# An mLSTM block's per-head weight subtraction: from VectorE to GpSimd

## The reference, cut to what matters

```
qk = silu(depthwise_conv5(concat[mq, mk]))          # q and k of a head
s  = (q @ k.T) * exp(decay matrix)                  # over chunks, two directions
h  = (s @ v) / max(|den|, exp(-m))                  # forward + backward
y  = rmsnorm(h) * g_mlstm * sigmoid(mo)             # mo = tokens @ w_in[:, o-columns]
```

## Time and profile before

| | us |
|---|---|
| median of 3 runs | 3441.33 |
| lowest, highest | 3435.79, 3441.35 |
| the profiled execution's own time | 3441.02 |
| its span, first to last instruction | 3439.2 |
| PE busy | 3324.5 (97%) |
| DVE busy | 2028.6 |
| ACT busy | 1232.1 |
| POOL busy | 357.2 |

### The profile page before, as it was taken

One profiled execution on the slowest core, in us unless ns is written; L12 is line 12 of the kernel. 1 busy time (PEld: TensorE's weight loads), 2 busy tenths in 40 slices (PEclk: granted clock), 3 DMA queues, 4 the chain that ended last, 5 costly groups with the idle time before them and its releaser, 6 DMA issues.

```text
span 3439.2 us, 42627 instructions
## 1 busy us (share of the span) xinstructions
PE 3324.5 (97%) x16432; PEld 2639.3 (77%) x16432; DVE 2028.6 (59%) x2501; ACT 1232.1 (36%) x1530; POOL 357.2 (10%) x334
## 2 busy tenths in 40 slices
PE   8999999999999998999998999999999999999999
PEld 4777768888887776688885587788887477878887
DVE  4676777555566576565567556465557566364443
ACT  3245443221224445432234433342224333343222
POOL 0000101110011001111112100011112011001000
PEclk9999999999999999999999999999999999999999
DMA  6331123323321222054442122244443132232223
GB/s 276 118 103 59 53 69 123 110 100 131 110 98 66 82 85 72 29 188 169 166 149 80 47 74 83 98 145 174 166 166 115 37 99 68 90 106 89 95 97 110
DMA packets 61017, 369.39 MB, mean 107 GB/s; under 512 B 9224, under 2 KB 9864, under 8 KB 19792
## 3 DMA queue, kind: packets, MB, share of 16 engines
q1 hardware_dynamic: 44544, 274.13, 23.0%
q10 hardware_dynamic: 16336, 93.39, 7.5%
HBM read 354.27 MB, written 2.33 MB: 104 GB/s over the span
## 4 chain that ended last, share of the span: by engine, by line
PE 80%; DVE 12%; ACT 5%; issue 3%; DMA 1%; POOL 0%; ACTq 0%; DVEq 0%; SPq 0%; POOLq 0%
PE pair L691 49%; PE pair L1163 8%; PE pair L842 6%; PE pair L729 2%; PE pair L759 2%; PE pair L1231 2%; PE pair L997 2%; DVE w_lo L2240 1%; PE pair L703 1%; ACT w_hi L1524 1%; PE pair L783 1%; PE pair L1059 1%; DVE mxg L2834 1%; PE pair L1362 1%; PE pair L1215 1%
## 5 line engine op out<-in xcount | busy, mean ns | idle before, releaser
L2240 DVE TENSOR_TENSOR w_lo<-raw,w_hi 128x2048 fp32r<-128x2048 f32 x221 | 506.9, 2294 | 285.2 <-ACT w_hi L1524 279.9
L1524 ACT ACTIVATE w_hi<-raw 128x2048 fp32r<-128x2048 f32 x221 | 421.7, 1908 | 622.6 <-PE pair L691 527.9
L691 PE MATMUL pair<-h_hi,w_hi 128*128 128x512 f32 (+2 forms) x1856 | 595.7, 363 | 5.7 <-DVEq L2222 2.7
L691 PE MATMUL pair<-h_lo,w_hi 128*128 128x512 f32 (+2 forms) x1856 | 594.5, 362 | 0.0
L691 PE MATMUL pair<-h_hi,w_lo 128*128 128x512 f32 (+2 forms) x1856 | 594.2, 362 | 0.0
L691 PE MATMUL pair<-u_hi,w_hi 128*128 128x512 f32 x1116 | 374.1, 371 | 19.1 <-DVE x L2281 10.1
L691 PE MATMUL pair<-u_lo,w_hi 128*128 128x512 f32 x1116 | 372.0, 369 | 0.0
L691 PE MATMUL pair<-u_hi,w_lo 128*128 128x512 f32 x1116 | 371.6, 368 | 0.0
L691 PEld LDWEIGHTS pair<-h_hi,w_hi 128*128 128x128 f32 (+2 forms) x1856 | 309.5, 183 | 67.5 <-issue 7.3
L2503 DVE TENSOR_TENSOR u_lo<-arena,u_hi 128x512 fp32r<-128x512 f32 (+1 forms) x128 | 97.1, 759 | 447.7 <-POOL arena L3047 447.4
L691 PEld LDWEIGHTS pair<-h_hi,w_lo 128*128 128x128 f32 (+2 forms) x1856 | 309.5, 183 | 61.3
(11 more groups left out here) (371 smaller groups left out, 4834.5 us busy)
## 6 DMA issues: line engine op xcount, KB each, us to landing
raw<-in_wt_dram SPq DMA_DIRECT2D x222, 1024.0 KB, 4.8
arena<-in_modw_dram ACTq DMA_DIRECT2D x72, 1024.0 KB, 4.9
arena<-in_modw_dram SPq DMA_DIRECT2D x12, 1024.0 KB, 9.6
raw<-in_modw_dram SPq DMA_DIRECT2D x12, 1024.0 KB, 4.8
arena<-arena SPq DMA_DIRECT2D x136, 64.0 KB, 2.0
arena<-negm_rows_dram ACTq DMA_DIRECT2D x16, 384.0 KB, 4.0
x<-in_xt_dram SPq DMA_DIRECT2D x1, 3072.0 KB, 18.6
arena<-in_fconst_dram ACTq DMA_DIRECT2D x2, 1414.0 KB, 6.4
```

Of the source, the lines that this page charges most:

```text
L691: mm = pe.matmul(pp[p][0:m, lo:hi], a[0:rows, k * width + c0:k * width + c0 + m], b[0:rows, k, lo:hi], start=(k == 0 and i == 0), stop=(k ...
L1524: act.activation(w_hi[slot][:], raw[slot][:], ACT.Copy).then_inc(w_hi_done, 1)
L2240: dve.tensor_tensor(w_lo[slot][:], raw[slot][:], w_hi[slot][:].bitcast(F32), ALU.subtract)\
```

## The change

In each head, the subtraction for the gate tile is done by POOL. DVE skips it (it only counts it, so that its later waits have the right values) and, before the `split()` inside the score loop, waits until that of the gate tile is complete. POOL does it first in each head, before its waits for the spread rows and for k. The tile indices are 6, 8, 10 and 12 in layer 0 and 56, 58, 60 and 62 in layer 1. POOL waits for the high part of this tile and for the low parts of all tiles before.

```diff
+            def split_elsewhere():
+
+                t.tile += 1
+                t.next("split")
+                t.next(w_hi_done)
+
...
                     convolve(h, 0)
-                    split()
+                    split_elsewhere()
                     if h:
...
                         if j == (2 if h < MH - 1 else 1):
+
+                            dve.wait_ge(w_lo_done, t.now(w_hi_done, 2))
                             split()
...
+            def split(i):
+
+                pool.wait_ge(w_hi_done, i + 1)
+
+                pool.wait_ge(w_lo_done, i + 2)
+                pool.tensor_tensor(w_lo[i % 2][:], raw[i % 2][:], w_hi[i % 2][:].bitcast(F32), ALU.subtract)\
+                    .then_inc(w_lo_done, 1)
+
             def mlstm(n):
...
                 for h in range(MH):
+                    split(6 + 2 * h if ctx_q else 56 + 2 * h)
 
                     pool.wait_ge(negm_in, t.next(negm_in, 32))
```

## The result

| | median us | lowest, highest | runs |
|---|---|---|---|
| before | 3437.49 | 3435.79, 3441.35 | 5 |
| after | 3454.75 | 3454.13, 3457.79 | 5 |
| ratio | 1.0043 | 95% interval 1.0029 to 1.0057 | |

The forecast was 8.0 us slower, 3449.0 us with a range up to 3453.5. So sign and mechanism came out as forecast, and the size was forecast too small.

A forecast was written before the change was run, and what follows sets the result against it. PE was taken to bound the kernel nearly everywhere (80% of the chain). Shifts reaching PE, 1.86 + 1.86 + 1.7 + 0.3 + 0.5 = 6.2 us, plus 1.8 of clock gave 8.0 on 3441.0: 3449.0 us, range 3443.0 to 3453.5.

The forecast's parts named there:

- the price of the hold: q-convolution: POOL's 4.49 us subtraction holds DVE's second scalar_tensor_tensor, which has two SBUF inputs, for 4.22 us.
- the 1.55 us of L2717: DVE tensor_tensor in the old trace: 2.233 us instead of 0.687 beside a 768-column POOL subtraction, used to size the hold.
- the net per head: DVE in each head: 4.22 us of wait less 2.36 us freed, +1.86 us, bounds +1.35 to +2.47.
- where PE feels it in layer 1: Layer 1: heads 1 and 2 pass on 1.86 us each, head 3 1.7 us, head 0 nothing.
- layer 0: Layer 0: of 1.86 us per head, 0.3 gets through in head 0, 0.5 in head 1, nothing in heads 2 and 3.
- 1.86 - 2.08 nothing: Layer 0, head 2: ACT's 1.03 and DVE's 1.05 us of waiting absorb the whole 1.86 us, 0 passed on.
- 1.86 - 1.40 leaves 0.5: Layer 0, head 1: ACT's 0.40 and DVE's 1.00 us of waiting leave 0.5 us passed on.
- the clock: Score loops of heads 1 and 2, layer 1, fall to head 3's level: 0.88 + 0.84, rounded up for layer 0, 1.8 us.
- DVE is not held: Rival at the q-convolution: DVE's second scalar_tensor_tensor goes ahead, DVE saves 2.36 us, 3434.7 to 3436.5 us; chance 0.10.
- A ceiling on the wait: Rival: DVE waits 1.55 us, once; heads 1 and 2 gain 0.81 us each, 3439.4 us; chance 0.06.
- Held, but soaked up: Rival: clock unchanged or score loop gives part of the shift back, 3445.5 us, between 3443.5 and 3448; chance 0.32.
- Longer: Variant: POOL takes 5.1 us, heads cost 2.47 us, low clock in layer 0 too, 3452.5 us; 0.52 together with the forecast.

The follow-up runs named there:

- the second measurement: The changed kernel itself, unchanged, run a second time beside a long series of the kernel before: 3452.38 us, ratio 1.0035.
- 768 columns: Changed kernel with POOL's subtraction cut to the 768 of 2048 columns that PE reads: 3436.97 us, ratio 0.9992.
- the right place: Against the kernel before: in layer 1, heads 1 to 3, high part and POOL's subtraction moved into the preceding score loop; head 0 as changed: 3435.16 us, 0.9981.
- the eight memsets of POOL: Changed kernel with a POOL memset of 128x2048, which reads nothing, in place of each subtraction: 3435.52 us, ratio 0.9982.

## Why the prediction was right, and what it mis-sized

**Right: the mechanism and the price of the hold.** The forecast of DVE's wait, 4.22 us, was measured as 7.33 - 3.10 = 4.23 in layer 1 and 5.24 - 1.02 = 4.22 us in layer 0. It came from one row, the 1.55 us of L2717, and from POOL's length put together out of two others: 4.49 us forecast, 4.56 measured where DVE's products stood beside it, and 4.75 with POOL's own wait for the first scalar_tensor_tensor, 4.83 as the mean of the eight (4.5 to 4.9 forecast, 4.62 to 5.08 in the single ones). That both terms of the wait fit to 0.01 us is luck in part: POOL took 0.07 us more than forecast, and the part of its length that does not hold DVE was 4.56 - 4.23 = 0.33 us, not 0.27. In head 0 of layer 1 the wait was 4.44 us. PE's wait in heads 1 and 2 of layer 1 was forecast as 4.1 us and is 4.03. The Trainium skill, page "GPSIMD Engine Reference", section "Elementwise — side-by-side cycle accounting", has 4497 ns for an addition of this length; the trace's 4.56 us agrees within 2%. That POOL gets in between two instructions of DVE that stand back to back, and that the second waits, is in the chain at 1202.14.

**Slightly low: the net per head.** Forecast 1.86 us, measured 2.02 (5.46 us became 7.48). The place of the subtraction had been taken as 2.36 us, from the end of the convolution at 1203.44 to the next copy. But 0.15 us of this is a gap that stands ahead of the copy in any case: 1208.84 - 1208.69 in after.

**Right: where PE feels it in layer 1.** Forecast 1.86, 1.86 and 1.7 us for heads 1 to 3. The start of the scores of chunk 1 is shifted by 2.02, 2.02 and 1.89 us more in each: 5.93 us, 5.4 forecast. The shift got through in head 3 as argued, as a wait of 1.60 us. The 0 of head 0 was right too, although DVE is held in it.

**Too low: layer 0.** Forecast 0.3, 0.5, 0 and 0 us. The shift grows by 0.56 us in head 0, by 0.45 in head 1, by 0.71 in head 2 (1.23, of which 0.52 come back in the loop), and falls by 0.3 after: 1.5 us in place of 0.8. The step that failed is "1.86 - 2.08 nothing" for head 2. It added up two slacks, ACT's 1.03 and DVE's 1.05 us, as if both lay ahead of PE. Only the first does. ACT's copy of the last head's output starts at 280.02 instead of 277.25, 2.38 us later besides the trace's shift of 0.39; less 1.03 that leaves 1.35, and PE waits 1.31 us before the scores of chunk 1. DVE's slack lies behind that, inside the loop, and gives 0.52 back. The sum for head 1, "1.86 - 1.40 leaves 0.5", has the same fault, and that it came out is luck: the copy starts at 236.86 instead of 235.49, 1.43 us late with the shift of -0.06 taken out; less 0.40 that leaves 1.03, PE waits 1.00 us, and 0.46 come back in the loop. It is only 1.43 us late, and not 2.02, because DVE came out of head 0's loop 0.6 us early (it starts the convolution at 210.40 instead of 211.07).

**Too low: the clock, and the stretch it was looked for in.** Forecast 1.8 us. In the three loops of layer 1 it was 2.13 + 0.60 - 0.56 = 2.2 us, close in sum by luck and wrong in its parts: the forecast let heads 1 and 2 rise to the level of head 3, 13.5 us, and left head 3 alone. They took 14.75 and 13.26 us, and head 3 fell by 0.56. Outside of the heads the forecast had nothing, and the stretch 1990 to 2060 lost 3.2 us in both traces of the changed kernel, with 0.90 for 0.97. That is the largest piece that was missed, and it is not shown to be the change's: the kernel with DVE's 768 columns and a filled wait loses the same 3.2 us there. What sets the clock in that stretch stays open. The last 2.1 us of the first trace did not repeat.

**The sum.** Heads of layer 0 1.5 us, of layer 1 5.93 + 2.2, less 1.1 that came back behind them (1322 to 1410 us), and 3.2 at 2000: 11.7 us by the trace, against 12.0 for the second measurement and 8.0 forecast. What was forecast, waits and clock in the heads, is 9.6 us of this; the 1.1 and the 3.2 are PE's clock in stretches where kernels without the hold show as much. Of the 5.3 us by which the first measurement has more, 2.9 are the kernel before's, whose median of 3437.49 in five runs is the lowest of its four (3440.46, 3440.39, 3443.20), and 2.4 the changed kernel's. The first median, 3454.75, lies 1.3 us above the range, the second inside it. The range's top took in 0.9 us more of clock and a longer POOL, and nothing for the spread of executions, though the three runs that were shown lay 5.6 us apart.

**The rivals.** *DVE is not held* was refuted by the 4.99 us. Its price of 3434.7 to 3436.5 us was right all the same: it is about what the kernels gave in which no hold reaches PE (3434.09, 3435.52, 3435.16). *A ceiling on the wait* fell with 1.45 us for 768 columns and 4.23 for 2048. *Held, but soaked up* at 3445.5 was too hopeful: the loops took more and not less. *Longer* at 3452.5 had the size, though not for its reason: POOL took 4.56 us by itself and not 5.1.

## What to carry to other kernels

Before an elementwise instruction goes to POOL, look at what DVE does in those microseconds: beside instructions with two inputs in SBUF it costs DVE nearly its whole length on POOL (4.2 of 4.56 us, for 2.3 saved), beside products out of PSUM it cost next to nothing (0.3 us on the tensor_scalar behind them). Look first whether the work is needed at all: cutting it to the columns that PE reads gave as much (0.9984) as moving it to the right place (0.9981), with a far smaller edit. And count a wait on PE about twice, once itself and once for the clock behind it, but take this for an average over stretches and not for a figure of each. And when two traces are compared, cut their windows at the same instructions and not at the same times.

## What was not expected of the hardware

- A head's clock is not its own. Behind waits of the same 3.50 us loops of the same instructions took 13.26 to 14.75 us at 0.83 to 0.70. In head 3 of layer 1, behind 2.56 us, the unchanged kernel had 0.76 in one execution and 1.00 in another.
- The clock can be low where nothing was changed: the same 3.2 us are lost at 1990 to 2060 by after and by a kernel without any subtraction on POOL.
- With a wait of 0.91 us ahead of it the loop of head 1 ran at 1.00, all at 2.4 GHz (10.97 us), with 2.25 us at 0.86, partly at 1.2 GHz (12.62 us), and with after's wait filled by unread matmuls at 1.00 again.
- Between executions of one program the time spreads by 18 us (3433.9 to 3451.9), and goes with the mean granted clock. Over the 97 runs of the kernel before that stood beside the experiments, the median span was 3434.9 us at a clock of 0.989, 3439.0 at 0.987 and 3446.7 at 0.985. Effects of 0.1 to 0.2% in this kernel can be read from the trace's own waits, not from a handful of times.
- An affine_select of POOL waits for DVE just as DVE for POOL, but the eight memsets of POOL took 1.81 us each and made none of the convolutions' instructions wait.
